# The modulation vectors of two layers as multiply-and-sum instructions on VectorE, and the mixers' low weight halves on GpSimd

## The reference, cut to what matters

```python
def first_block(x, c, ...):                      # DEPTH = 2
    c_act = jax.nn.silu(c)                       # (1, 1024)
    for l in range(DEPTH):
        mod = (c_act @ ada_w[l] + ada_b[l])      # (1024) @ (1024, 6144): 48 columns of 128
        sh1, sc1, g1, sh2, sc2, g2 = split(mod, 6)
        h = rmsnorm(x, norm_mix_w[l]) * (1 + sc1) + sh1
        x = x + g1 * mixer(h, ...)
        h = rmsnorm(x, norm_ffn_w[l]) * (1 + sc2) + sh2
        x = x + g2 * conv_ffn(h, ...)
    return rmsnorm(x, final_norm_w)
# the second block: mod_l = silu(c_2) @ w_ada + b_ada for the 256 latent tokens,
#                   mod_c = silu(c_ctx_2) @ w_ada + b_ada for the 256 context tokens (their first 16 columns are used)
```

## Time and profile before

| | |
|---|---|
| median of 3 runs | 2246.31 us (2245.22 to 2254.6) |
| span of the profiled execution | 2240.1 us |
| PE busy | 1996.3 us (89%) |
| DVE busy | 1435.2 us (64%) |
| ACT busy | 1096.0 us (49%) |
| POOL busy | 144.5 us (6%) |
| moved by DMA | 447.54 MB, mean 200 GB/s |

### The profile page before, as it was taken

One profiled execution on the slowest core, in us unless ns is written; L12 is line 12 of the kernel. 1 busy time (PEld: TensorE's weight loads), 2 busy tenths in 40 slices (PEclk: granted clock), 3 DMA queues, 4 the chain that ended last, 5 costly groups with the idle time before them and its releaser, 6 DMA issues. The chain is left out here.

```text
span 2240.1 us, 36916 instructions
## 1 busy us (share of the span) xinstructions
PE 1996.3 (89%) x15254; PEld 1676.1 (75%) x15254; DVE 1435.2 (64%) x1795; ACT 1096.0 (49%) x1328; POOL 144.5 (6%) x150
## 2 busy tenths in 40 slices
PE   5788899899788889899969895798899999999998
PEld 5586677799677667699868764686778788788786
DVE  0264345787355444678645948755788788788786
ACT  0353343565254334455446533212567677676674
POOL 0000000000000000000002613630000000000000
PEclk8799799899999879999989997899899999999999
DMA  9764264445276337354432210000679899799797
GB/s 382 275 220 149 94 218 150 188 188 179 91 254 211 111 107 253 131 208 177 143 145 83 75 55 11 14 19 12 231 282 376 303 347 378 265 370 375 275 376 268
DMA packets 154104, 447.54 MB, mean 200 GB/s; under 512 B 10080, under 2 KB 12768, under 8 KB 151392
## 3 DMA queue, kind: packets, MB, share of 16 engines
q1 hardware_dynamic: 153952, 445.41, 55.1%
HBM read 444.33 MB, written 1.05 MB: 199 GB/s over the span
## 5 line engine op out<-in xcount | busy, mean ns | idle before, releaser
L212 DVE TENSOR_TENSOR me_wlow<-me_w,me_whigh 128x2048 fp32r<-128x2048 f32 (+1 forms) x203 | 451.8, 2247 | 105.1 <-ACT me_whigh L207 104.9
L207 ACT ACTIVATE me_whigh<-me_w 128x2048 fp32r<-128x2048 f32 (+1 forms) x203 | 380.2, 1885 | 135.4 <-PE ps L220 126.1
L218 PE MATMUL ps<-me_whigh,me_xhigh 128*128 128x512 f32 x512 | 207.1, 405 | 12.0 <-PEq L119 12.0
L218 PE MATMUL ps<-up_xhigh,ffn_whigh 128*128 128x256 f32 x704 | 201.8, 287 | 8.6 <-DVE ffn_wlow L212 7.0
L220 PE MATMUL ps<-me_whigh,me_xlow 128*128 128x512 f32 x528 | 208.4, 395 | 0.0
L219 PE MATMUL ps<-me_wlow,me_xhigh 128*128 128x512 f32 x512 | 201.9, 394 | 0.0
L219 PE MATMUL ps<-up_xlow,ffn_whigh 128*128 128x256 f32 x704 | 200.9, 285 | 0.0
L220 PE MATMUL ps<-up_xhigh,ffn_wlow 128*128 128x256 f32 x704 | 200.8, 285 | 0.0
L212 DVE TENSOR_TENSOR ffn_wlow<-ffn_w,ffn_whigh 128x2048 fp32r<-128x2048 f32 (+1 forms) x72 | 149.3, 2110 | 60.8 <-ACT ffn_whigh L207 60.6
L212 DVE TENSOR_TENSOR mix_wlow<-mix_w,mix_whigh 128x1024 fp32r<-128x1024 f32 (+2 forms) x116 | 140.2, 1213 | 69.2 <-ACT mix_whigh L207 69.0
L207 ACT ACTIVATE ffn_whigh<-ffn_w 128x2048 fp32r<-128x2048 f32 (+1 forms) x72 | 123.2, 1759 | 47.8 <-PE ps L220 47.8
(11 more groups left out here) (658 smaller groups left out, 4208.2 us busy)
## 6 DMA issues: line engine op xcount, KB each, us to landing
me_w<-w_exp_gate SPq DMA_DIRECT2D x34, 2048.0 KB, 9.6
me_w<-w_exp_up SPq DMA_DIRECT2D x34, 2048.0 KB, 10.1
me_w<-w_exp_down SPq DMA_DIRECT2D x32, 2048.0 KB, 10.1
mix_w<-w_mix SPq DMA_DIRECT2D x108, 512.0 KB, 4.3
mix_aside<-ada_w SPq DMA_DIRECT2D x96, 512.0 KB, 4.3
ffn_w<-ffn_w_up SPq DMA_DIRECT2D x20, 2048.0 KB, 8.1
ada_w<-ada_first SPq DMA_DIRECT2D x12, 2048.0 KB, 23.2
ffn_w<-ffn_w_down SPq DMA_DIRECT2D x8, 2048.0 KB, 7.8
```

The lines of the kernel that those rows point to most:

```text
L207: return nc.scalar.activation(high, x, ACT.Copy)
L212: return nc.vector.tensor_tensor(low, x, high.bitcast(F32), ALU.subtract)
L218: nc.tensor.matmul(out, lh, rh, start=start, stop=False)
```

## The change

1. `opening` makes only the first 16 modulation columns of layer 0 (`NEXT`), in 8 transfers of 1 MB, all with slots of their own. The weights lie transposed in memory: a piece holds 128 results on the partitions and the 1024 weights of each along the row. The row c comes by a transfer that repeats it on all 128 partitions; ScalarE takes its silu; VectorE multiplies each piece with that row and sums, one instruction a piece (`add_up`), and adds the bias.
2. In each mixer 64 pieces are fetched and summed in the same way: the other 32 columns of this layer (`CURRENT`), the first 16 of the next, and 16 of the second block (`OTHER`). Their instructions stand in VectorE's queue at even planned steps of about 2.7 us from 11.0 on, with a pause of 5 us ahead of each new row c. SP fetches them into three slots. TensorE, and ScalarE but for three silus, have no part in it.
3. In each FFN 8 more pieces are summed (`LATE`), one for each chunk of the up product from the third on, through one slot, with one silu on ScalarE.
4. The mixer's low weight halves are made by GpSimd (`low_parts_apart`) and no longer by VectorE.
5. The mixer's products use four banks of PSUM in turn, not three; the norm waits for one copy more.

```diff
+CURRENT, NEXT, OTHER, LATE = 32, 16, 16, 8
+class Modulation:
+    def fetch_row(self, sp, s):
+        if s:
+            sp.wait_ge(self.used, self.firsts[s])
+        sp.dma_start(self.row, self.sets[s][1].to_broadcast([P, DM])).then_inc(self.row_here, 16)
+    def fetch(self, sp, j):
+        if j >= self.slots:
+            sp.wait_ge(self.used, (j - self.slots + 1) * self.together)
+        a = j * self.together
+        sp.dma_start(self.ring[:, j % self.slots], self.w[a:a + self.together].rearrange("q p f -> p q f"))\
+            .then_inc(self.landed[j % self.slots], 16)
+    def bend(self, nc, act, s):
+        act.wait_ge(self.row_here, 16 * (s + 1))
+        nc.scalar.activation(self.row, self.row, ACT.Silu).then_inc(self.row_ready, 1)
+    def add_up(self, nc, dve, i):
+        j, q = divmod(i, self.together)
+        if i in self.firsts:
+            dve.wait_ge(self.row_ready, self.firsts.index(i) + 1)
+        dve.wait_ge(self.landed[j % self.slots], 16 * (j // self.slots + 1))
+        w = self.ring[:, j % self.slots, q, :]
+        nc.vector.scalar_tensor_tensor(out=w, in0=w, scalar=1.0, in1=self.row, op0=ALU.mult, op1=ALU.mult,
+                                       accum_out=self.sums[:, i:i + 1]).then_inc(self.used, 1)
+    def finish(self, nc, dve, s):
+        count, _, bias, out = self.sets[s]
+        a = self.firsts[s]
+        dve.wait_ge(self.used, a + count)
+        nc.vector.tensor_tensor(out, self.sums[:, a:a + count], bias, ALU.add).then_inc(self.made, 1)
 # opening
-    n = ADA_PIECES // 4
-    slots, banks, middle_at = 5, 4, 4
+    together, middle_at = 2, 3
+    n = NEXT // together
 ...
+                ada.fetch_row(sp, 0)
                 for j in range(n):
+                    ada.fetch(sp, j)
+                    if j == 0:
+                        sp.dma_start(bias_to, bias_from).then_inc(bias_here, 16)
                     if j == middle_at:
                         for to, source in middle:
                             sp.dma_start(to, source).then_inc(middle_here, 16)
-                for to, source in last:
+                for to, source in first + last:
                     sp.dma_start(to, source).then_inc(last_here, 16)
 ...
+                for i in range(NEXT):
+                    ada.add_up(nc, dve, i)
+                    if i == 2 * middle_at + 5:
                         angles()
+                ada.finish(nc, dve, 0)
 # Pieces
+    def low_parts_apart(self, nc, pool):
+        for p, when in enumerate(self.split_at()):
+            yield when + 1.2
+            pool.wait_ge(self.high, p + 1)
+            nc.gpsimd.tensor_tensor(self.halves(p)[1], self.whole(p), self.halves(p)[0].bitcast(F32), ALU.subtract)\
+                .then_inc(self.low, 1)
 # mixer
-        pieces.clock = 3.5
-        for _ in range(4):
-            modulation_piece(0.9)
-        pieces.clock = max(pieces.clock, 11.0)
-        for n, (name, i, cost) in enumerate(order):
+        pieces.clock = 11.0
+        for name, i, cost in order:
             if (name, i) == ("out", 0):
                 pieces.clock += 1.0
             weights(name, i, cost)
-            for _ in range((1, 1, 1, 1, 0, 1, 1, 2, 0)[n % 9]):
-                modulation_piece()
-        units = Units(core, sem, "mix", 3, names)
+        banks = 4
+        units = Units(core, sem, "mix", banks, names)
+        ada_from, ada_gap = 11.0, 5.0
+        ada_step = (pieces.clock - 14.0 - ada_from - 2 * ada_gap) / ada.n
+        def ada_at(i):
+            return ada_from + ada_step * i + ada_gap * sum(i >= first for first in ada.firsts[1:])
+        def ada_fetch(sp):
+            for j in range(ada.n):
+                yield ada_at(j - ada.slots) + 1.5 if j >= ada.slots else 3.0 * j
+                if j == 0:
+                    ada.fetch_row(sp, 0)
+                if j - ada.slots + 1 in ada.firsts[1:]:
+                    ada.fetch_row(sp, ada.firsts.index(j - ada.slots + 1))
+                ada.fetch(sp, j)
+        def ada_dve(dve):
+            for s, (count, *_) in enumerate(ada.sets):
+                for i in range(ada.firsts[s], ada.firsts[s] + count):
+                    yield ada_at(i)
+                    ada.add_up(nc, dve, i)
+                yield ada_at(ada.firsts[s] + count - 1) + 1.5
 ...
+                ada.finish(nc, dve, s)
         def spread_dve(dve):
+            dve.wait_ge(ada.made, 1)
 ...
-                in_turn(setup_dve(dve), norm_dve(dve), pieces.low_parts(nc, dve), lat_read_dve(dve), lat_dve(dve),
+                in_turn(setup_dve(dve), norm_dve(dve), lat_read_dve(dve), lat_dve(dve),
+            @block.gpsimd
+            def _(pool):
+                in_turn(pieces.low_parts_apart(nc, pool))
 # ffn
+            ada.bend(nc, act, 0)
             for n in range(2 * FF_TILES):
 ...
+                if n % 4 == 1 and n // 4 in range(2, 2 + LATE):
+                    ada.add_up(nc, dve, n // 4 - 2)
 ...
                     if n >= STAGES:
                         sp.wait_ge(low, before(n - STAGES + 1))
+                    if n == STAGES:
+                        ada.fetch_row(sp, 0)
+                        ada.fetch(sp, 0)
+                    elif n in range(STAGES + 4, STAGES + 3 + LATE):
+                        ada.fetch(sp, n - STAGES - 3)
```

More of the change, by code:

```diff
@@ L487, in _ @@
                             sp.dma_start(to, source).then_inc(middle_here, 16)
-                for to, source in last:
+                for to, source in first + last:
                     sp.dma_start(to, source).then_inc(last_here, 16)
[L490 to L513, removed]
-                pe.wait_ge(silu, 1)
-                for j in range(n):
-                    share(j)
-                    if j >= 2:
-                        add_up(j - 2)
-                add_up(n - 2)
-                add_up(n - 1)
@@ L783, in fetch @@
[L783 to L805 removed]
+        pe.wait_ge(self.low, p + 1)
@@ new lines, in fetch @@
+    def fetch(self, sp, between=None):
+        planned = self.split_at()
+        for p in range(len(self.rows)):
+            yield planned[p - self.raws] + 2.0 if p >= self.raws else 1.5 * p + 1.0
+            if between and p in between:
+                between[p]()
+            if p >= self.raws:
+                sp.wait_ge(self.low, p - self.raws + 1)
+            sp.dma_start(self.whole(p), self.rows[p][2]).then_inc(self.landed[p % self.raws], 16)
+    def split_at(self):
+        out = []
+        for p, at in enumerate(self.at):
+            when = at - self.lead
+            if p >= self.raws:
+                when = max(when, out[p - self.raws] + 1.7)
+            if p >= self.parts:
+                when = max(when, self.at[p - self.parts] + 0.5)
+            out.append(when)
@@ L1108, in tokens @@
                 return mm
-            for p, (name, i, _, n, _) in enumerate(pieces.rows):
+            for p, (name, i, _, n) in enumerate(pieces.rows):
                 yield pieces.at[p]
                 pieces.arrived(pe, p)
-                if name == "ada":
-                    if i == 0:
-                        pe.wait_ge(silu, 1)
-                    ada_share(pe, i, pieces.whole(p)).then_inc(done, 1)
-                    continue
                 w = pieces.halves(p)
```

317 lines of the change are left out of this document (110 added, 207 removed).

## The result

The changed kernel takes 2225.4 us (median of 4 runs, 2224.7 to 2226.1) against 2246.5 of the kernel before on the same chip: a ratio of 0.9912, 95% interval [0.9884, 0.9940]. It is faster, by 0.9% where 3.8% was forecast: the time lies at the very end of the stated range, 2120 to 2226, and 65 us above the forecast of 2160. The profiled execution has a span of 2222.9 us.

What follows compares the result with a forecast made beforehand. The opening was taken as bound by transfers, the mixers mostly by TensorE, the FFN's up product by TensorE alone. 2240.1 - 43.5 - 46 + 3 = 2153.6 us span, plus 6.2 for the median: 2160 us, range 2120 to 2226.

Steps and rivals of the forecast that it cites:

- The opening, -43.5: Opening: with only 16 sums, VectorE's chain of sums, angles and bias ends it at 33.2 instead of 76.5 us.
- The price of a sum: VectorE's multiply with summed output over 1024 columns: taken as 1.35 us, near the plain instruction's 1.226.
- The rival of a sum at half rate: All stages: the summed output halves the rate, a sum takes 2.4 us, 2289 us in all; chance 0.12.
- The start, -3.5: Start of each mixer, where x is normalised: TensorE no longer waits behind modulation pieces; 3.5 us saved.
- The FFNs, +1.5 each: Each FFN: a sum fits the 11.5 us chunk, but later weights cost 1.5 us; ends 0 and +8.
- The later stretches of the mixers, -2, -8 and -10: Second, third and fourth stretches of each mixer: 2, 8 and 10 us saved as TensorE loses modulation work.
- the second stretch: Mixer stretch dense in weights, 80 us before: VectorE sets it at 78, or -2.
- the third stretch: Mixer stretch with attention and mLSTM, 120 us before: GpSimd and VectorE have room; -8.
- the two engines eat the mixers' gain: Rival: more GpSimd-VectorE meetings and late evacuations hold TensorE; mixers +5, FFNs +5, 2223 us; chance 0.18.
- the fourth stretch: Mixer stretch again dense in weights, 96 us before: 86 us expected, or -10.
- three signs of error: A sum takes 2 us; GpSimd needs over 3.3 on fp32r outputs; SP's queue holds weights behind sums.
- the mixers' term: Each mixer: 23 us saved, -46 for both; ends 0 and -40 a mixer.

Runs made afterwards that it cites:

- e4: Changed kernel plus a stage behind the opening running six of each kind of instruction alone and side by side; run once, 2382.9 us in all, only that stage's trace used.
- e7: Changed kernel with GpSimd's low-half subtraction cut to 64 columns, so most low halves are left out; 2127.7 us, ratio 0.9476 to the kernel before.
- e1: Changed kernel with the mixers' low halves made by VectorE again, sums still 1,024 columns; 2183.4 us, ratio 0.9736 to the kernel before.
- e3: Changed kernel with low halves back on VectorE and the mixers' sums cut to 64 columns; 2143.2 us, ratio 0.9549 to the kernel before.
- e6: Low halves on VectorE, sums' ring of two slots, GpSimd making 58 subtractions a mixer that nobody reads; 2397.7 us, ratio 1.0691 to the kernel before.
- e12: Changed kernel with sums over 512 columns, three banks for the mixers' products and the sums' row in PSUM; 2175.3 us, ratio 0.9701 to the kernel before.

## Why the prediction was wrong

**The opening, -43.5:** it was -43.2, and it ends in the chain that was named, sums, then bias. To the half microsecond that is luck, though: the 16 sums start 1.15 us apart and not 1.35, which saves 3.2 us, and VectorE waits 3.8 us for transfers between them, 2.60 of it ahead of the ninth, which the term put at nothing (the first pair is there 0.9 us early).

**The price of a sum.** The rival of a sum at half rate is out: 1.22 us alone, in the opening, the FFN (1.225) and `e4`. The Trainium skill's point on two SBUF sources that are not bf16 (Vector Engine (DVE) Microarchitecture Reference, Points that are easy to get wrong), that they halve the rate, did not hold for this instruction with its summed output: 1,024 columns take what the plain instruction takes.

**The start, -3.5:** it was -2.6.

**The FFNs, +1.5 each:** the first came out at -2.2 (210.6 to 208.4), the second at +1.3 between the same two instructions. The chunk of 11.5 us had room for a sum, as reckoned.

**The later stretches of the mixers, -2, -8 and -10: this is the step that failed.** They were +17, -19 and +15. Two things were wrong in the dense ones, the second and the fourth.

*The price.* "VectorE needs 51.5 - 22.4 = 29 of other work, 24 x 1.35 and 24 x 0.6" prices a collision for the sums alone. For them it was nearly right: 0.72 us each where 0.6 was taken (the prediction's own two thirds and half an instruction give 0.79). But VectorE's other instructions were held as well. VectorE is busy 85.3 us in the second stretch where 76 was reckoned, and 85.4 in the fourth where 67 was. The account for a whole mixer stands in the last column of the experiments' table. With next to nothing on GpSimd (`e7`) VectorE works 166.5 us. Making the low halves itself (`e1`) it works 59.4 more. With them on GpSimd it works 65.7 more: 45.4 in the sums (123.3 against 77.9 in `e1`) and some 20 in its other instructions. The engine that was to be relieved is as busy as if it had made the low halves itself, 232 us against 226.

*The overlap.* The prediction took a stretch to last as long as its busiest engine, and 2 to 3 us more. The second stretch lasts 97.4 us with VectorE busy 85.3, and the fourth 111.1 with TensorE busy 86.6 and VectorE 85.4: 12 and 25 us more, since VectorE's results come late one by one and TensorE waits for them. In part it is so without a collision too. `e1` in the same two stretches:

```profile
51.20:135.30 84.10, 64.89 (x393) 57.90 (x392) 74.54 (x144) 47.32 (x77) 0.00 (x0) 0.92 0.74 255
242.00:339.60 97.60, 83.57 (x353) 67.15 (x352) 78.98 (x117) 39.83 (x48) 0.00 (x0) 0.90 0.71 248
```

That is 10 and 14 us more than the busiest engine has. The waits also show in TensorE's clock: the changed kernel's dense stretches have 0.86, with TensorE idle 28 and 25 us of them, where the kernel before has 0.98 and 1.00 with 6 and 4 us idle, and TensorE is busy 69.1 and 86.6 us where 66 and 82 were reckoned. In the third stretch it is the other way: TensorE's busy time fell by 21 us, not 14, at a granted clock of 0.90 and not 0.82.

**The rule was applied to the sums alone.** The prediction read 1.68 us for a pair of 512, 0.90 of a full block, and took 3.3 for a pair of 1024. `e4` shows 3.55 us for a sum and a subtraction of 1,152, which alone take 1.22 and 2.57: 0.94 of a full block. The Trainium skill (SBUF — State Buffer, Who interferes with whom) has it that the second of such a pair blocks fully, and the trace nearly agrees. The Trainium skill also says there that a VectorE instruction with one SBUF input is free of it, but not in the two-port modes. The sum with its row in PSUM at 1.22 us agrees, and the `TENSOR_SCALAR` of one SBUF input fits the second half: it takes 0.28 us alone, where a product of two operands of that size takes 0.40, and 2.42 beside GpSimd. A full block of the sums alone, 7 us more in each dense stretch by the prediction's working, would not have mended the forecast: 28 us more are 2188. What was missing is that the block meets the short instructions as well, for up to the whole of GpSimd's 2.4 to 2.6 us, and that these stand in front of TensorE.

**The rival that came true** is the second, "the two engines eat the mixers' gain", 2223 us, with a chance of 0.18. Its mechanism, more meetings and late results, is what the runs show. That its number is right to 2 us is luck: its mixers of +5 were +11.9 and +11.6 from mark to mark, its FFNs of +5 were -3.2 and +1.3, and the second block, which it left alone, was +5.0. "Against it: GpSimd idles in the third stretch" was true, with GpSimd busy 27.6 of 100.5 us, and that stretch did gain, but not what the other two lost.

**What had been named as signs.** A sum alone at 1.3 to 1.4 and up to 3.4: 1.22, and up to 3.42 in the mixers (3.62 in `e4`). Low halves on GpSimd of 2.4 to 3.3: 2.75 on average. TensorE's idle in the fourth stretch ended by low halves: it was not, they held it 0.3 us in both mixers together. None of the three signs of error that had been named came about: ScalarE waited only 6 and 7 us for `mix_w` in the two mixers behind their start.

**What is left of the mixers' term.** Without GpSimd (`e1`) a mixer is 322.2 - 312.7 = 9.5 us shorter, still not 23. The sums' own work on VectorE takes the rest: with sums of 64 columns (`e3`) it is 28.4. Once a collision-free engine took the low halves (`e7`), it would be 38.5 with all sums in place.

**Lateness, and what is open.** That GpSimd's low halves are late rather than in the way explains little of the 40 us: TensorE's matmuls wait 0.3 us for them behind the mixers' starts, its weight loads 6.7 us in seven waits. The second block, whose code is the same in all kernels, took 1103.5 to 1109.7 us in the 14 profiles, and TensorE's busy time in it went with the granted clock: 990.2 us at 0.947 in the kernel before, 997.7 at 0.937 in the changed one, 999.1 at 0.934 in `e6`. So its 5 us here go with the clock; why the clock differs between runs of the same code stays open. How much each held instruction is worth at the end, by its place, was not measured. A row of full length in PSUM, which needs two banks, and a fourth slot in the ring, for which there was no room, were not tried.

## What to carry to other kernels

Work moved from VectorE to GpSimd is to be charged against all VectorE instructions that read two operands from SBUF, and short ones of one operand like the `TENSOR_SCALAR` here, and not only against the new or long ones: each that meets GpSimd pays about what is left of GpSimd's instruction, and here 59 us of relief cost 66 in each mixer. Nor is a stretch as long as its busiest engine: where two engines hand results to each other one by one, here 10 to 25 us came on top. Before such a move look at where VectorE's operands lie, since with one of them in PSUM nothing was lost here. Transfers that an in-order engine waits for at the head of its queue want their full ring: one slot of three was worth 37 us.

## What the runs showed of the hardware

- A multiply with a summed output over 1,024 fp32 columns from two SBUF operands takes 1.22 us, and 0.08 more for the read of the accumulator, which overlaps its neighbours (a start every 1.15 us).
- VectorE and GpSimd in turns on SBUF (`e4`): one of each every 3.55 us, where they take 1.22 and 2.57 alone. An instruction of 64 columns loses as much (0.69 us on average) as one of 1,024 (0.72).
- A `TENSOR_SCALAR` with a single SBUF input of 8x256, 0.28 us alone, took 2.42 beside GpSimd; a copy from PSUM (0.61) and a sum with its row in PSUM (1.22) took no longer.
- GpSimd's subtraction into fp32r takes 2.57 us for 1,152 columns. Its mean in the mixer, most of them 1,024 wide, is 2.43 us where the sums have their row in PSUM (`e12`) and 2.75 in the changed kernel, where VectorE holds it in turn.
- The same 1,168 matmuls of the first mixer keep TensorE busy 236.3 us at a granted clock of 0.92 (`e7`), 243.9 at 0.90 (`e1`), 246.5 at 0.88 (changed) and 272.9 at 0.82 (`e6`).
